# Attention by head pairs on halves of TensorE's array, instead of head by head

## The reference, cut to what matters

```python
s = einsum(q, k) * HEAD_DIM ** -0.5      # HEAD_DIM = 64
p = joint_softmax([s_win + mask_or_bias, s_ctx], sink)
o = einsum(p, v)
```

## Time and profile before

| | us |
|---|---|
| median of 3 runs | 2592.52 |
| fastest, slowest run | 2589.06, 2595.80 |
| span of the profiled execution | 2587.8 |
| PE busy | 2439.7 |
| PE weight loads busy | 1968.7 |
| DVE busy | 1746.4 |
| ACT busy | 1344.9 |
| POOL busy | 64.5 |

### The profile page before, as it was taken

The page is one execution under the profiler, slowest core; times in us unless marked ns, Lnnn a source line. Parts: engine busy times, 40 slices in busy tenths (PEclk is TensorE's granted clock), DMA queues, the critical chain, the costliest instruction groups (busy, mean ns, idle before and its releaser), DMA issues.

```text
span 2587.8 us, 34710 instructions
## 1 busy us (share of the span) xinstructions
PE 2439.7 (94%) x12344; PEld 1968.7 (76%) x12344; DVE 1746.4 (67%) x2249; ACT 1344.9 (52%) x1636; POOL 64.5 (2%) x123
## 2 busy tenths in 40 slices
PE   6999999999799999979999969999999999999997
PEld 3767877777578788757888858888888888888885
DVE  5565444643555335466546549898989898989897
ACT  5344444432444233234435437676767676767675
POOL 0000010100000000000011000000000000000000
PEclk8999999999899999989999979999999999999999
DMA  6222332233144334313233529998989898989894
GB/s 222 73 91 98 114 106 90 98 117 138 39 164 160 104 140 162 104 60 107 92 112 120 174 102 356 342 352 335 359 333 365 327 364 329 368 325 370 325 367 166
DMA packets 128777, 528.62 MB, mean 204 GB/s; under 512 B 9136, under 2 KB 68016, under 8 KB 75440
## 3 DMA queue, kind: packets, MB, share of 16 engines
q1 hardware_dynamic: 126096, 520.86, 54.8%
q10 hardware_dynamic: 2592, 6.55, 0.8%
HBM read 526.33 MB, written 1.05 MB: 204 GB/s over the span
## 4 chain that ended last, share of the span: by engine, by line
PE 87%; DVE 7%; ACT 3%; issue 2%; DMA 1%; DVEq 0%; ACTq 0%; SPq 0%
PE O L1623 11%; PE pp L1289 9%; PE pp L1290 9%; PE pp L1291 9%; PE S L1601 8%; PE S L1599 8%; PE S L1600 8%; PE pp L1313 3%; PE O L1377 3%; PE S L1359 2%; PE T L1387 2%; PE S L1289 1%; PE S L1290 1%; PE T L1290 1%; PE S L1291 1%
## 5 line engine op out<-in xcount | busy, mean ns | idle before, releaser
L850 DVE TENSOR_TENSOR wsp<-raw,wsp 128x1024 fp32r<-128x1024 f32 (+3 forms) x344 | 379.3, 1127 | 485.0 <-ACT wsp L568 480.8
L1236 DVE TENSOR_TENSOR opr<-M,opr 128x2048 fp32r<-128x2048 f32 x168 | 383.5, 2287 | 29.9 <-ACT opr L798 27.1
L568 ACT ACTIVATE wsp<-raw 128x1024 fp32r<-128x1024 f32 (+3 forms) x344 | 322.6, 966 | 122.1 <-PE T L1291 82.0
L798 ACT ACTIVATE opr<-M 128x2048 fp32r<-128x2048 f32 x168 | 322.6, 1920 | 91.8 <-PE O L1623 52.0
L1599 PE MATMUL S<-opr,hx 128*128 128x512 f32 x896 | 358.9, 401 | 2.3 <-DVE hx L1241 2.2
L1601 PE MATMUL S<-opr,hx 128*128 128x512 f32 x896 | 350.3, 391 | 0.0
L1600 PE MATMUL S<-opr,hx 128*128 128x512 f32 x896 | 349.4, 390 | 0.0
L1623 PE MATMUL O<-opr,wsp 128*128 128x512 f32 x1344 | 311.4, 391 | 13.0 <-DVE opr L1236 13.0
L1289 PE MATMUL pp<-hx,wsp 128*128 128x512 f32 (+1 forms) x800 | 286.5, 358 | 26.6 <-DVE hx L932 14.8
L1623 PEld LDWEIGHTS O<-opr,wsp 128*128 128x128 f32 x1344 | 250.5, 188 | 67.7 <-DVE opr L1236 16.3
L1290 PE MATMUL pp<-hx,wsp 128*128 128x512 f32 (+1 forms) x800 | 277.4, 347 | 0.0
(11 more groups left out here) (205 smaller groups left out, 3537.6 us busy)
## 6 DMA issues: line engine op xcount, KB each, us to landing
M<-in_w_moe SPq DMA_DIRECT2D x168, 1024.0 KB, 4.9
raw<-in_w_main SPq DMA_DIRECT2D x132, 1024.0 KB, 4.9
raw<-in_w_moe SPq DMA_DIRECT2D x114, 1024.0 KB, 5.0
xm<-in_w_moe SPq DMA_DIRECT2D x56, 1024.0 KB, 5.7
raw<-in_w_br SPq DMA_DIRECT2D x24, 512.0 KB, 3.5
raw<-in_w_dn SPq DMA_DIRECT2D x8, 768.0 KB, 4.2
raw<-in_w_dn SPq DMA_DIRECT2D x8, 640.0 KB, 3.9
M<-in_rpb_rows ACTq DMA_DIRECT2D x16, 256.0 KB, 3.4
```

What stands on the lines that cost most here:

```text
L568: act.activation(wsp[:, slot, 0, 0:w], raw[:, slot // 2, half * w:half * w + w], ACT.Copy).then_inc(hi_done, 1)
L798: act.activation(wse[i % SPLIT_E][:, 0, :, :], raw_e[i % RAW_E], ACT.Copy).then_inc(e_hi, 1)
L850: dve.tensor_tensor(wsp[:, slot, 1, 0:w], raw[:, slot // 2, half * w:half * w + w], wsp[:, slot, 0, 0:w], ALU.subtract).then_inc(lo_done, 1)
L1236: dve.tensor_tensor(w[:, 1, :, :], raw_e[i % RAW_E], w[:, 0, :, :], ALU.subtract).then_inc(e_lo, 1)
```

## The change

A slot now holds a pair: both heads of one tile and block of queries. There are 48 pairs, and `spread` is given pairs plus 3 slots instead of units plus 4, so 19 slots instead of 36 in each branch of layer 0, and 11 instead of 20 in layer 1.

- The padded tile `q2`, POOL's copies and their semaphore go. POOL only adds the column mask to the bias, head after head.
- The scores of a head use its own 64 rows of queries and keys, so its weights lie in one half of the array's rows. The keys are cut in two column halves `c`, and the four matmuls of a pair alternate between the heads, with bank `S[0]` and `S[1]` for them.
- The value matmuls of the two heads alternate as well. Each used its own 64 columns of the array before too, but all of one head's stood together.
- At slot s, PE does scores of pair s, values of pair s-2, transposes of pair s-1. Before, the transposes were two slots behind the scores.
- DVE does its normalising of pair s-1 first and then mask and maximum of pair s; before the order was the other way.
- PE waits for the exponentials of both units of the pair before. The bias of a pair's heads is loaded when the second block of queries (qt 1) of the tile before is at ACT.

```diff
-            units = (nq // P) * 8
+            pairs = (nq // P) * 4
...
-            flow += [([(0, k) for k in sl], s) for sl, s in spread(steps[head:mid], units + 4)]
-            flow += [([(1, k) for k in sl], s) for sl, s in spread(steps[mid:end], units + 4)]
+            flow += [([(0, k) for k in sl], s) for sl, s in spread(steps[head:mid], pairs + 3)]
+            flow += [([(1, k) for k in sl], s) for sl, s in spread(steps[mid:end], pairs + 3)]
...
-            return [(tt, half, qt) for tt in range(4) for half in range(2) for qt in range((TOK if l == 0 else SEQ) // P)]
+            return [(tt, qt, half) for tt in range(4) for qt in range((TOK if l == 0 else SEQ) // P) for half in range(2)]
...
-                        wait_taken(pool, step_of[l, "rope_q" if b == 0 else "qn", tt])
-                        if w >= 2:
-                            pool.wait_ge(scores_done, w - 1)
-                        src = (qa if b == 0 else qn)[64 * half:64 * half + 64, tt, P * qt:P * qt + P]
-                        pool.tensor_copy(q2[64 * half:64 * half + 64, half, w % 2, :], src).then_inc(q2_ready, 1)
...
                 nqt = (TOK if l == 0 else SEQ) // P
-                if s < len(units):
-                    tt, half, qt = units[s]
-                    w = unit_base[l, b] + s
-                    n = TOK if qt < 2 else SEQ
-                    sc = st[:, w % 4, :]
-                    bank = S[w % 2]
-                    dve.wait_ge(scores_done, w + 1)
...
+                for half in range(2):
+                    n = 2 * (s - 1) + half
+                    if 0 <= n < len(units):
+                        w = unit_base[l, b] + n
+                        N = TOK if units[n][1] < 2 else SEQ
+                        sc = st[:, w % 4, :]
+                        dve.wait_ge(exp_done, w + 1)
                         if b == 0:
+                            own.link(dve.tensor_tensor(sc[:, 2:3], sc[:, 2:3], sc[:, 3:4], ALU.add))
+                        own.link(dve.reciprocal(sc[:, 4:5], sc[:, 2:3]))
+                        dve.tensor_scalar(pr[:, half, 0:N], pr[:, half, 0:N], sc[:, 4:5], None, ALU.mult).then_inc(probs_done, 1)
+                for half in range(2):
+                    n = 2 * s + half
+                    if n < len(units):
+                        tt, qt, _ = units[n]
+                        w = unit_base[l, b] + n
+                        N = TOK if qt < 2 else SEQ
+                        sc = st[:, w % 4, :]
+                        bank = S[half]
...
-                if 0 <= s - 1 < len(units):
-                    w = unit_base[l, b] + s - 1
-                    n = TOK if units[s - 1][2] < 2 else SEQ
-                    sc = st[:, w % 4, :]
-                    dve.wait_ge(exp_done, w + 1)
-                    if b == 0:
-                        own.link(dve.tensor_tensor(sc[:, 2:3], sc[:, 2:3], sc[:, 3:4], ALU.add))
-                    own.link(dve.reciprocal(sc[:, 4:5], sc[:, 2:3]))
...
-                if s < len(units):
-                    tt, half, qt = units[s]
-                    w = base + s
-                    pe.wait_ge(q2_ready, w + 1)
+                if 2 * s < len(units):
+
+                    tt, qt, _ = units[2 * s]
+                    w = base + 2 * s
+                    wait_taken(pe, step_of[l, "rope_q" if b == 0 else "qn", tt])
                     if w >= 2:
-                        pe.wait_ge(exp_done, w - 1)
+                        pe.wait_ge(exp_done, w)
                     if b == 0:
                         wait_taken(pe, step_of[l, "rope_k", 0])
-                        keys = ka
+                        q, keys = qa[:, tt, P * qt:P * qt + P], ka
                     else:
                         wait_taken(pe, step_of[l, "kn", tt])
-                        keys = kn[:, tt, :]
+                        q, keys = qn[:, tt, P * qt:P * qt + P], kn[:, tt, :]
                     k0 = 0 if qt < 2 else SEQ
-                    mm(S[w % 2][:, 0:TOK - k0], q2[:, half, w % 2, :], keys[:, k0:TOK], start=True, stop=True
-                       ).then_inc(scores_done, 1)
-                if 0 <= s - 3 < len(units):
-                    w = base + s - 3
-                    tt, half, qt = units[s - 3]
+                    N = (TOK - k0) // 2
+                    for c in range(2):
+                        for half in range(2):
+                            h = slice(HD * half, HD * half + HD)
+                            ins = mm(S[half][:, N * c:N * c + N], q[h, :], keys[h, k0 + N * c:k0 + N * c + N], start=True, stop=True)
+                            if c == 1:
+                                ins.then_inc(scores_done, 1)
+                if 0 <= 2 * (s - 2) < len(units):
+                    tt, qt, _ = units[2 * (s - 2)]
+                    w = base + 2 * (s - 2)
                     kts = range(4) if qt < 2 else range(2, 4)
                     ot = otile_base[l, b] + tt
-                    pe.wait_ge(pT_copied, w + 1)
-                    if half == 0 and qt == 0 and ot >= 2:
+                    pe.wait_ge(pT_copied, w + 2)
+                    if qt == 0 and ot >= 2:
                         pe.wait_ge(o_split, ot - 1)
-                    if s - 3 == 0:
+                    if s - 2 == 0:
                         if b == 0:
                             wait_taken(pe, step_of[l, "va_t", 0])
                         else:
                             for key in ((0, 0), (0, 1), (1, 0), (1, 1)):
                                 wait_taken(pe, step_of[l, "vn", key])
-                    vc = HD * half if b == 0 else P + HD * (2 * tt + half)
                     for n, k in enumerate(kts):
-                        ins = mm(O[ot % 2][HD * half:HD * half + HD, P * qt:P * qt + P], V[:, k, vc:vc + HD],
-                                 prT[:, w % 2, n, :], start=(n == 0), stop=(n == len(kts) - 1))
-                    ins.then_inc(pv_done, 1)
-                if 0 <= s - 2 < len(units):
-                    w = base + s - 2
-                    kts = 4 if units[s - 2][2] < 2 else 2
-                    pe.wait_ge(probs_done, w + 1)
-                    if w >= 2:
-                        pe.wait_ge(pT_copied, w - 1)
-                    for k in range(kts):
-                        ins = pe.transpose(T[w % 2][:, P * k:P * k + P], pr[:, w % 2, P * k:P * k + P], ident[:])
-                    ins.then_inc(pT_done, 1)
+                        for half in range(2):
+                            vc = HD * half if b == 0 else P + HD * (2 * tt + half)
+                            ins = mm(O[ot % 2][HD * half:HD * half + HD, P * qt:P * qt + P], V[:, k, vc:vc + HD],
+                                     prT[:, half, n, :], start=(n == 0), stop=(n == len(kts) - 1))
+                            if n == len(kts) - 1:
+                                ins.then_inc(pv_done, 1)
+                if 0 <= 2 * (s - 1) < len(units):
+                    qt = units[2 * (s - 1)][1]
+                    kts = 4 if qt < 2 else 2
+                    for half in range(2):
+                        w = base + 2 * (s - 1) + half
+                        pe.wait_ge(probs_done, w + 1)
+                        if w >= 2:
+                            pe.wait_ge(pT_copied, w - 1)
+                        for k in range(kts):
+                            ins = pe.transpose(T[half][:, P * k:P * k + P], pr[:, half, P * k:P * k + P], ident[:])
+                        ins.then_inc(pT_done, 1)
```

More of the change, by code:

```diff
@@ L196, in build_program @@
         sd = view(M, 11776, TOK)
-        q2 = view(M, 12288, 2, 2, P)
         gt = view(M, 12800, 2, TOK)
@@ L530, in _ @@
             for l in range(2):
[L531 to L536, removed]
-                        tt, half, qt = units[s]
-                        w = unit_base[l, b] + s
-                        if b == 1 and s == 0:
-                            mask_bias(l, 0)
-                        wait_taken(pool, step_of[l, "rope_q" if b == 0 else "qn", tt])
-                        if w >= 2:
-                            pool.wait_ge(scores_done, w - 1)
-                        src = (qa if b == 0 else qn)[64 * half:64 * half + 64, tt, P * qt:P * qt + P]
-                        pool.tensor_copy(q2[64 * half:64 * half + 64, half, w % 2, :], src).then_inc(q2_ready, 1)
-                        pool.wait_ge(q2_ready, w + 1)
-                        if b == 1 and qt == nq // P - 1 and s + 1 < len(units):
-                            mask_bias(l, 2 * tt + half + 1)
+                for head in range(8):
+                    mask_bias(l, head)
             pool.wait_ge(routed, 1)
@@ L647, in attn @@
-                if s < len(units):
-                    tt, half, qt = units[s]
-                    w = unit_base[l, b] + s
-                    n = TOK if qt < 2 else SEQ
-                    sc = st[:, w % 4, :]
-                    act.wait_ge(pre_done, w + 1)
-                    if b == 1 and qt == 0 and 1 <= 2 * tt + half < 7:
-                        load_bias(l, 2 * tt + half + 1)
```

(21 more changed lines are left out.)

71 lines of the change are left out of this document (35 added, 36 removed).

## The result

The changed kernel takes 2633.65 us (median of 4 runs, 2628.65 to 2638.48); the kernel before, on the same chip, 2591.55 (2589.06 to 2595.8). The ratio is 1.016 (95% 1.0147 to 1.0173): slower by 42 us. Forecast were +16 us, 2608, with a range of 2562 to 2632. The sign was right and the time lies 1.7 us above the range. Times are medians of a kernel's undisturbed executions; of experiment 4 the profiled execution was not one of them (4452.75 us, the other four 2836.19 to 2841.8), so none of its rows are read.

A forecast was written before the change was run, and what follows sets the result against it. TensorE was taken to set the pace, with a DVE and ACT chain beside it without slack in branch A. The terms -58 + 55 + 14 + 5 = +16 us on 2592.5 gave about 2608 us, range 2562 to 2632.

The forecast's parts named there:

- TensorE's gain: Scores and values of 48 pairs: the two heads' matmuls overlap on the array, saving 58 us.
- the right end: Of two bounds on TensorE's scores and values, the one where heads overlap: 58 us saved instead of 7.
- no overlap: Rival for scores and values: heads' matmuls run one behind another, gain only 7 us; +39, 2631 us, chance 0.19.
- Waits for the normalising: Attention slots: transposes wait for DVE to normalise in the same slot, behind the previous step's eviction; +55 us.
- The weights' chain: Four `ada` steps in layer 0: the next projection waits for weights split behind the whole slot; +14 us.
- The clock: TensorE's matmuls behind long waits run at the lower clock level; 4 of twelve such slots counted, +5 us.
- POOL's copies: POOL's padded copies hold nothing up, so removing them changes the time by 0.
- Faster: Rival: TensorE's gain stays, waits for DVE and weights together cost under 58 us; -29, 2563 us, chance 0.25.
- The test lines: Forecast wrong if transposes' waits stay under 30 us, a pair's scores take 1.9 us, or stretches without attention move.

The follow-up runs named there:

- experiment 4: The kernel before, with only the transposes one slot earlier (unit s-1 in slot s instead of unit s-2): 2841.43 us, ratio 1.0961.
- kernel 1: The changed kernel, with DVE normalising a pair at the start of the step behind its slot, ahead of that step's eviction: 2550.42 us, ratio 0.9839.
- experiment 6: kernel 1 with both heads' scores on rows 0 to 63 and both heads' values on all 128 columns: 2596.02 us, ratio 1.0004.
- Experiment 2: The changed kernel, with 281 useless matmuls in front of transposes that wait, so that TensorE stays busy: 2609.05 us, ratio 1.0061.
- experiment 7: The changed kernel with both heads' scores on rows 0 to 63 and both heads' values on all 128 columns: 2645.47 us, ratio 1.0199.
- experiment 5: kernel 1 with head 0's score and value matmuls all ahead of head 1's, not alternated: 2565.78 us, ratio 0.9887.

## Why the prediction was right in sign and short in size

Point by point, by its own steps:

- **TensorE's gain, 58 us: right, a little low.** The overlap exists, and I took the right end. Measured were 60 us in the changed kernel and 72 in kernel 1, where fewer matmuls ran at the lower clock. Scores of a long pair were forecast at 1.25 us and took 1.06; values were forecast at 1.13 and took 1.02. The picture behind it was wrong: I let one head's second pass run beside the other's first (five beats for eight passes), but both heads' passes start as a pair, 7 ns apart, and the pairs start at 0, 0.32, 0.54 and 0.75 us: four beats. In a short pair I let eight weight loads set the pace of the scores, 0.83 + 0.18 us (and took 136 ns for a load of 64 columns where the earlier trace rows has 137); they took 0.65, so no such limit showed. The other end, no overlap, was forecast at 3.80 us for a long pair, and experiment 6 measured 1.92 + 1.89 = 3.81.
- **Waits for the normalising, +55 us: right.** Idle time before transposes grew by 64: 28 in layer 0's branch A (forecast 28), 21 in its branch C (18), 10 in layer 1's branch C (9), and 5.4 in layer 1's branch A, for which I had nothing in the list. The kinds fit: 1.1 plus 0.2 us behind `gb` (1.2), 3.5 behind `ada` (3.7), 2.5 to 3.2 behind `gc` (2.6). Rows of three slots, `gc`, `gc` and `gb`:

```profile
150.37 1.90 PE L1384 MATMUL T<-ident,M 128*128 128x128 f32 x8 [2.63 <-DVE M L965]
175.18 1.34 PE L1384 MATMUL T<-ident,M 128*128 128x128 f32 x4 [2.51 <-DVE M L965]
191.65 1.44 PE L1384 MATMUL T<-ident,M 128*128 128x128 f32 x8 [1.11 <-DVE M L965]
```

- **The weights' chain, +14 us: right in kind, a third too high.** Four waits behind early `ada` steps make 10.9 us (the row above with 3.51 is one), less today's 2.0: +9, where four times 3.9 was forecast and 2.7 came on average. All other idle time together grew by 10.
- **The clock, +5 us: this is the step that failed.** The prediction said "Between none and all, 0 to 17 us, I take 4 of them, 5 us, since TensorE works on both sides of each wait." Measured are 34 us on other work and 12 more on the attention (135.9 against 123.7 in kernel 1; a small part of the 12 is not clock, since values that are followed by a wait count 0.07 us more), 46 in all. The clock record bounds it from above: unrounded, the share of the clock that was not granted comes to 53 and 35 us in the two mixers, before to 13 and 22, so 54 more, a part of which fell into waits where it cost nothing. Both factors of the term were too small. In the attention of both layers the clock fell 20 times, against twice before (outside the attention the two mixers have seven falls in either trace), so 18 more, not 4 more; and these falls lasted 4.8 us on average, some 11 matmuls at 0.43 us rather than my seven. The reason that I gave protected no wait: there were 14 waits of 2.5 us or more (twelve were forecast), and each had a fall at it or within 2 us behind. The other six falls stood at waits of 2.1 to 2.4 us, which I had not counted, though one of before's two falls stood behind waits of 0.80 and 1.99 us. Two windows, behind a wait of 2.63 us and behind one of 2.36:

```profile
150.00:154.00 4.00, 3.57 (x18) 2.42 (x19) 2.12 (x8) 2.23 (x7) 0.00 (x0) 0.60 0.00 0
1380.00:1384.00 4.00, 4.00 (x24) 4.00 (x23) 1.75 (x5) 2.23 (x6) 0.76 (x1) 0.62 0.47 122
```

  No length of a wait decides it by itself: in kernel 1 a wait of 2.58 us had no fall and one of 1.91 had. Experiment 2 shows the cause: with filler in the waits, 25 us came back.
- **POOL's copies, 0: right.** POOL fell from 63 to 27 us in the windows above, and no wait names it now, where before it held 0.2.

The sum with measured terms: -72 + 64 + 10 + 46 = +48 (rounded; the table's sums differ by 49.2), and the span grew by 48.6. The rivals: "no overlap" was priced at +39; measured in experiment 7 it is +52, short by its clock term as well (other work 21 us above before, where it allowed 3). "Faster" needed the waits under 58 us together, and they were 74. The test lines held: the waits of the transposes grew by 64 us where 55 were forecast, a long pair's scores were not 1.9 us, and the parts without attention moved by 2 us or less.

## What to carry to other kernels

Price the waits that a change adds by what they cost afterwards as well: here 74 us of new idle time on TensorE brought some 46 us more, because the same matmuls then ran at the lower clock. Before making TensorE faster, look at what the engine behind it has to finish in the shorter time. Here one edit to DVE's order turned +42 us into -41, and a second one made it -54, while TensorE's saving in the attention was of the same kind in all three (60, 72 and 71 us).

## What the hardware did that I had not expected

- Matmuls on different 64 rows, and on different 64 columns, of the array ran fully side by side: the starts are 6 to 7 ns apart in pairs, and eight passes of 256 columns take 1.06 us where the same count on the same rows took 1.92 us (experiment 6, scores of a long pair).
- The second head's matmuls started past those of the first that stood ahead of them in the queue, but not past any number. With four passes of head 0 ahead of it, head 1's first matmul started 13 ns after head 0's first. With eight passes ahead, it started 0.49 us later, together with head 0's fifth pass (values of experiment 5: the single starts are 240.36 and 240.85). So leaving out the alternation cost nothing in the scores and 0.5 us in long values.
- The falling clock cost 46 us on top of 74 us of new idle time. In layer 0's mixer the falls came 20 times in 687 us with waits spread over the slots, 8 times in 620 us with most of them gone, and 4 times in 640 us in the kernel before.
